# Cached pages laid out by transfers inside SBUF and turned on VectorE, half of a convolution's taps on GpSimd

## What is computed

```python
PAGE_SIZE, KV_LORA, QK_ROPE, N_HEADS, CONV_WIDTH = 128, 256, 32, 16, 31   # 16 pages per sample

def _mla_keys(kv_lat, k_rope, w_uk, g_k_head):
    k_nope = jnp.einsum('btl,lhd->bthd', kv_lat, w_uk)
    k_r = jnp.broadcast_to(k_rope[:, :, None, :], k_nope.shape[:-1] + (QK_ROPE,))
    return _rmsnorm(jnp.concatenate([k_nope, k_r], axis=-1), g_k_head)

# for every page of a sample (kv_blk: 128 tokens x 256, kr_blk: 128 tokens x 32)
k = _mla_keys(kv_blk, kr_blk, w_uk, g_k_head)
sc = jnp.einsum('bshd,bphd->bhsp', qf, k) * scale
# softmax over all pages and the new token, then
acc = jnp.einsum('bhsp,bpl->bhsl', p, kv_blk)

# the convolution of the prompt: 31 taps, each a shifted copy of z times a weight per channel
y = lax.conv_general_dilated(buf, w_dw[:, None, :], ..., feature_group_count=CONV_CH) + b_dw
```

## Time and profile before

| | |
|---|---|
| Median of three runs | 1144.9 us |
| The profiled execution | 1145.37 us |
| Its span on the core | 1143.5 us |
| Busy, share of the span: TensorE, VectorE, ScalarE, GpSimd | 98%, 68%, 51%, 6% |
| Granted TensorE clock, mean | 0.997 |
| Page stage | about 393 to 811 us |

### The profile page before, as it was taken

One profiled execution on the slowest core, in us unless ns is written; L12 is line 12 of the kernel. 1 busy time (PEld: TensorE's weight loads), 2 busy tenths in 40 slices (PEclk: granted clock), 3 DMA queues, 4 the chain that ended last, 5 costly groups with the idle time before them and its releaser, 6 DMA issues.

```text
span 1143.5 us, 25908 instructions
## 1 busy us (share of the span) xinstructions
PE 1122.7 (98%) x9549; PEld 1086.8 (95%) x9549; DVE 778.4 (68%) x1325; ACT 581.7 (51%) x1153; POOL 67.8 (6%) x136
## 2 busy tenths in 40 slices
PE   5999999999999999999999999999999999999998
PEld 3899999999898899999999999999999999999998
DVE  4655553567777688888888888888757666555543
ACT  3444453346576655455545454554566545444432
POOL 2000000010000100101010110101020010000000
PEclk9999999999999999999999999999999999999999
DMA  9987578947344440021211202032257684555552
GB/s 324 314 292 269 183 254 289 348 167 222 99 142 127 133 133 2 20 65 33 52 47 36 62 22 73 13 84 71 57 150 254 227 272 131 183 183 177 177 184 71
DMA packets 165629, 169.84 MB, mean 149 GB/s; under 512 B 25780, under 2 KB 144071, under 8 KB 165525
## 3 DMA queue, kind: packets, MB, share of 16 engines
q1 hardware_dynamic: 163799, 166.83, 45.6%
q10 hardware_dynamic: 1742, 1.88, 0.5%
HBM read 167.13 MB, written 2.49 MB: 148 GB/s over the span
## 4 chain that ended last, share of the span: by engine, by line
PE 92%; DVE 2%; SPq 2%; ACT 1%; DMA 1%; issue 1%; POOL 0%; DVEq 0%; ACTq 0%
PE PS L1894 27%; PE PS L1895 27%; PE PS L1896 27%; PE PS L1971 2%; SPq L451 2%; PE PS L2367 1%; PE PS L2342 1%; PE PS L2343 1%; DMA raw<-in_w_ffn_in 1%; PE PS L2288 1%; PE PS L2099 1%; PE PS L2308 0%; PE PS L2338 0%; DVE wL L1172 0%; PE PS L2287 0%
## 5 line engine op out<-in xcount | busy, mean ns | idle before, releaser
L1172 DVE TENSOR_TENSOR wL<-raw,wH 128x1024 fp32r<-128x1024 f32 (+2 forms) x208 | 246.3, 1191 | 209.8 <-ACT wH L717 208.4
L717 ACT ACTIVATE wH<-raw 128x1024 fp32r<-128x1024 f32 (+2 forms) x208 | 213.2, 1029 | 245.6 <-PE PS L1896 224.7
L1894 PE MATMUL PS<-uH,wH 128*128 128x264 f32 x1024 | 294.2, 287 | 4.5 <-DVE uL L1233 4.0
L1895 PE MATMUL PS<-uL,wH 128*128 128x264 f32 x1024 | 291.8, 285 | 0.0
L1896 PE MATMUL PS<-uH,wL 128*128 128x264 f32 x1024 | 291.4, 285 | 0.0
L1894 PE MATMUL PS<-wqH,kTH 128*128 128x336 f32 (+2 forms) x768 | 255.7, 333 | 0.0
L1896 PE MATMUL PS<-wqH,kTL 128*128 128x336 f32 (+2 forms) x768 | 246.1, 320 | 0.0
L1895 PE MATMUL PS<-wqL,kTH 128*128 128x336 f32 (+2 forms) x768 | 245.9, 320 | 0.0
L1894 PEld LDWEIGHTS PS<-uH,wH 128*128 128x128 f32 x1024 | 193.9, 189 | 7.9 <-issue 6.4
L1895 PEld LDWEIGHTS PS<-uL,wH 128*128 128x128 f32 x1024 | 194.2, 190 | 0.0
L1896 PEld LDWEIGHTS PS<-uH,wL 128*128 128x128 f32 x1024 | 193.6, 189 | 0.0
(11 more groups left out here) (343 smaller groups left out, 1497.8 us busy)
## 6 DMA issues: line engine op xcount, KB each, us to landing
raw<-in_w_ffn_in SPq DMA_DIRECT2D x86, 512.0 KB, 3.5
adaw<-in_w_ada SPq DMA_DIRECT2D x72, 512.0 KB, 6.5
raw<-in_w_ffn_out SPq DMA_DIRECT2D x32, 512.0 KB, 3.5
raw<-in_w_in SPq DMA_DIRECT2D x32, 512.0 KB, 4.5
kv<-in_cache_kv_latent SPq DMA_DIRECT2D x128, 128.0 KB, 2.0
raw<-in_w_ffn_out SPq DMA_DIRECT2D x16, 384.0 KB, 3.0
raw<-in_w_attn_out SPq DMA_DIRECT2D x8, 512.0 KB, 4.1
raw<-in_w_conv_out SPq DMA_DIRECT2D x8, 512.0 KB, 4.7
```

The costliest lines, as they stand in the source:

```text
L717: f(wH[:, k, 0:width], raw[:, k, 0:width], ACT.Copy).then_inc(w_hi, 1)
L1172: v.tensor_tensor(wL[:, k, 0:width], raw[:, k, 0:width], wH[:, k, 0:width].bitcast(F32), ALU.subtract).then_inc(w_lo, 1)
L1894: mm(dst, a[0], b[0], start=start, stop=False)
L1895: mm(dst, a[0], b[1], start=False, stop=False)
```

## The change

- Pages of sequences 1 to 7 are no longer turned by TensorE (`turn` leaves lines 2342 and 2343 out unless `turned`, which holds for sequence 0 only). Instead, for each group of four pages, SP issues four transfers inside SBUF (`blocks`): transfer q takes 32 channels of each half of the four pages, 8 pieces of 32 values (128 bytes) from each of the 128 partitions of `kv2`, and writes them to 32 partitions of a new tile `kx`, 1024 values in each. That is 1024 pieces for a transfer and 4096 for a group. VectorE then turns all blocks of 32 x 32 of `kx` by one instruction on 128 x 1024 into `kT32` (`turn_group`), before `page_lo` of pages 2, 6, 10 and 14, for the group that begins two pages later. `kx` and `kT32` have two slots each and lie where `raw` lies.
- ScalarE (`page_hi`) and VectorE (`page_lo`) read the turned page from `kT32` in SBUF, with an access pattern that puts the tokens in order; the pattern of `kTH` and `kTL` has a step of four values.
- New semaphores: `kx_in` (a group has landed), `kx_ps` (a group is turned), `kr_ps` (rope keys turned and multiplied), which ScalarE, VectorE and GpSimd wait for where they waited for `kT_ps` or `kTH_done`.
- SP's loop over page groups is written out: `sequence_loads(b)` mixes the page loads of the next sequence with the transfers of `blocks`. It starts only after the first gate quad has been split (`w_lo`), and the gate weights of quads 1 to 3 are loaded only after the last `kTL`.
- VectorE does taps 0 to 15 of each tile. GpSimd does taps 16 to 30: a product with the weight (broadcast along the row) and a sum into `yp`, 29 instructions of 128 x 256, in parts of 5, 4, 3 and 3 taps between its other work, and in `conv_sum` one more sum that adds `yp` to the tile.
- `VALUES_PAGE` goes from 10 to 8.

```diff
-VALUES_PAGE = 10
-TAPS = (0, 1, 1, 0, 2, 2, 1, 2, 2, 2, 7, 3, 2, 3, 1, 2)
-TAPS_FIRST = (2, 3, 3, 0, 2, 3, 0, 3, 3, 0, 3, 3, 0, 2, 2, 2)
+VALUES_PAGE = 8
+TAPS = (0, 0, 0, 0, 1, 1, 0, 1, 3, 1, 1, 2, 2, 2, 1, 1)
+TAPS_FIRST = (1, 2, 1, 0, 1, 1, 0, 1, 2, 0, 1, 2, 0, 1, 2, 1)
+DVE_TAPS = sum(TAPS)
+POOL_TAPS = (DVE_TAPS, DVE_TAPS + 5, DVE_TAPS + 9, DVE_TAPS + 12, CW)
...
+        kx = sb("kx", [P, 2, 4 * KL], at=ring)
+        kT32 = sb("kT32", [P, 2, 4 * KL], at=ring + 8192)
+        yp = sb("yp", [P, SEQ], at=gains)
+        ytmp = sb("ytmp", [P, SEQ], at=taps_at)
...
+        def turned_page(n):
+            return kT32[:, n // 4 % 2, :].rearrange("p (k a h t) -> p a h k t", k=4, a=4, h=2)[:, n % 4, :, :, :]
...
+            def pages_next(b, g):
+
+                sp.wait_ge(pg_rel, 4 * b + g + 1)
+                page_group(b, b % 2, g)
+
+            def blocks(b, g):
+
+                grp = 4 * (b - 1) + g
+                sp.wait_ge(kv2_in[4 * (b % 2) + g], 128 * (b // 2) + 128)
+                if grp >= 2:
+                    sp.wait_ge(kx_ps, grp - 1)
+                pages = kv2[:, NPG * (b % 2) + 4 * g:NPG * (b % 2) + 4 * g + 4, :].rearrange(
+                    "p a (h q i) -> p (a h) q i", q=4, i=QUAD)
+                for q in range(4):
+                    sp.dma_start(kx[QUAD * q:QUAD * q + QUAD, grp % 2, :], pages[:, :, q, :]).then_inc(kx_in[grp % 2], 16)
+
+            def sequence_loads(b):
+
+                if b >= 1:
+                    blocks(b, 2)
+                    blocks(b, 3)
+                if 1 <= b < NB - 1:
+                    pages_next(b + 1, 0)
+                if b < NB - 1:
+                    blocks(b + 1, 0)
+                if 1 <= b < NB - 1:
+                    pages_next(b + 1, 1)
+                    pages_next(b + 1, 2)
+                if b < NB - 1:
+                    blocks(b + 1, 1)
+                if 1 <= b < NB - 1:
+                    pages_next(b + 1, 3)
...
-            with sp.Fori(1, 4) as i:
-                sample_pages(i, 0)
-                sample_pages(i, 1)
+            sp.wait_ge(w_lo, 4 * Q_GATE + 4)
+            for b in range(NB):
+                sequence_loads(b)
+            sp.wait_ge(kTL_done, PAGES + 2)
             with sp.Fori(1, 4) as i:
                 gate_quad(i)
...
             def conv_sum(f_):
 
                 pool.wait_ge(tap_done, f_ + 1)
+                own.wait()
+                own.done(g.tensor_tensor(u[:, f_, 0:SEQ], u[:, f_, 0:SEQ], yp[:, :], ALU.add))
+                own.wait()
...
+            def taps(f_, part):
+
+                for t in range(POOL_TAPS[part], POOL_TAPS[part + 1]):
+                    z, w = zbuf[:, f_, t:t + SEQ], wdw[:, f_, t:t + 1].to_broadcast([P, SEQ])
+                    own.wait()
+                    if t == DVE_TAPS:
+                        own.done(g.tensor_tensor(yp[:, :], z, w, ALU.mult))
+                    else:
+                        own.done(g.tensor_tensor(ytmp[:, :], z, w, ALU.mult))
+                        own.wait()
+                        own.done(g.tensor_tensor(yp[:, :], yp[:, :], ytmp[:, :], ALU.add))
...
+            for b in range(NB):
+                taps(b, 0)
+                if b >= 1:
+                    score_max(b - 1)
+                taps(b, 1)
+                if b >= 1:
+                    new_probabilities(b - 1)
+                taps(b, 2)
+                rope_square(b)
+                taps(b, 3)
                 if b < NB - 1:
                     conv_sum(b)
                     sample_rows(b + 1)
+            score_max(NB - 1)
+            new_probabilities(NB - 1)
             conv_sum(NB - 1)
...
-            def page_hi(pg, n):
-                act.wait_ge(kT_ps, pg + 1)
+            def page_hi(b, n, turned=False):
+                pg = NPG * b + n
+                if turned:
+                    act.wait_ge(kT_ps, n + 1)
+                else:
+                    act.wait_ge(kx_ps, 4 * b + n // 4 - 3)
                 act.wait_ge(kn_ps, pg + 1)
...
+                if turned:
+                    f(kTH[:, n % 2, :], PS[:, 0, 0:KL], ACT.Copy).then_inc(kTH_done, 1)
+                else:
+                    f(kTH[:, n % 2, :].rearrange("p (h t k) -> p h k t", h=2, k=4), turned_page(n), ACT.Copy
+                      ).then_inc(kTH_done, 1)
...
+            def turn_group(b, g):
+
+                dve.wait_ge(kx_in[g % 2], 128 * b + 64 * (g // 2) - 64)
+                dve.wait_ge(kTL_done, NPG * b + 4 * g - 2)
+                v.transpose(kT32[:, g % 2, :], kx[:, g % 2, :]).then_inc(kx_ps, 1)
...
+                    v.tensor_tensor(lo_.rearrange("p (h t k) -> p h k t", h=2, k=4), turned_page(n),
+                                    hi_.rearrange("p (h t k) -> p h k t", h=2, k=4), ALU.subtract
+                                    ).then_inc(kTL_done, 1)
...
                 for n in range(NPG):
                     pg = NPG * b + n
+                    if n % 4 == 2:
+                        if n + 2 < NPG:
+                            if not first:
+                                turn_group(b, (n + 2) // 4)
+                        elif not last:
+                            turn_group(b + 1, 0)
                     if not (last and n == NPG - 1):
-                        page_lo(pg + 1, (n + 1) % NPG, b, s, first)
+                        page_lo(pg + 1, (n + 1) % NPG, b, s, first, first and n + 1 < NPG)
...
-                tr(PS[:, 0, 0:128], kv2[:, NPG * s + n, 0:128], ident)
-                tr(PS[:, 0, 128:256], kv2[:, NPG * s + n, 128:256], ident).then_inc(kT_ps, 1)
+                if turned:
+                    tr(PS[:, 0, 0:128], kv2[:, NPG * s + n, 0:128], ident)
+                    tr(PS[:, 0, 128:256], kv2[:, NPG * s + n, 128:256], ident).then_inc(kT_ps, 1)
```

More of the change, by code:

```diff
@@ L169, in decoder_layer @@
         vecT = sb("vecT", [P, V_N])
+        gains = base[0]
         gbc = sb("gbc", [P, B_N])
@@ L356, in decoder_layer @@
         kv2_in = [sem(f"kv2_in{g}") for g in range(8)]
+        kx_ps, kr_ps = sem("kx_ps"), sem("kr_ps")
+        kx_in = [sem(f"kx_in{g}") for g in range(2)]
         qx_done, den_ps, mx_done, gmx_done, sub_done, p_done, lsum_done = map(
@@ L665, in conv_sum, with rope_square @@
                     g.tensor_tensor(ysum[:, :], ysum[:, :], u[:, f_, :], ALU.add).then_inc(ysum_done, 1)
-            pool.wait_ge(st_sb, 4)
-            sample_rows(0)
-            for b in range(NB):
-                pool.wait_ge(kTH_done, NPG * b + 14)
+            def taps(f_, part):
[8 more added lines that the diff above has]
+                        own.done(g.tensor_tensor(yp[:, :], yp[:, :], ytmp[:, :], ALU.add))
+            def rope_square(b):
+                pool.wait_ge(kr_ps, 8 * b + 7)
                 if b >= 1:
@@ L1054, in sequence @@
                     pg = NPG * b + n
-                    if not (last and n == NPG - 1):
-                        page_hi(pg + 1, (n + 1) % NPG)
+                    if n + 1 < NPG:
+                        page_hi(b, n + 1, first)
+                    elif not last:
+                        page_hi(b + 1, 0)
                     if n == 1 and not first:
```

49 lines of the change are left out of this document (27 added, 22 removed).

## The result

| | before | after |
|---|---|---|
| Median | 1144.7 us | 1161.3 us (four runs, 1157.9 to 1164.7) |
| Ratio after to before, 95% interval | | 1.0148 [1.0116, 1.0181] |
| The profiled execution, its span | 1145.37, 1143.5 us | 1164.70, 1162.6 us |
| Granted TensorE clock, mean | 0.997 | 0.990 |

The account below looks back on a forecast made before the run. TensorE, busy 98% of the span, was taken as the bound. Its -24.6 us, plus 5 (lock and heavy pages), 6 (transfers) and 2 (start), gave -11.6: a median of 1133 us, range 1120 to 1155, with 1126 to 1141 at 50%.

Parts of the forecast that it names:

- The 24.6 us from TensorE: Pages 16 to 127: 112 page transpositions of 0.22 us leave TensorE, all on the path; a sequence would last 48.8 us.
- Clean: Rival 1: pieces at 7 to 13 ns, VectorE in time, only 2 us at the start remain: 1122 us; chance 17%.
- kTL at 0.42: VectorE's subtraction in each page, now from SBUF with a stride, left at 0.42 us, bounds 0.35 and 0.6.
- The lock: GpSimd and VectorE block each other at shared SBUF ports: 36 exposed operations, 4.5 us more VectorE per sequence.
- the heavy pages: VectorE at pages 2, 6, 10, 14, with the lock: 0.7 us per sequence reaches TensorE, 5 us, bounds 0 and 25.
- The transposition: VectorE's new 128x1024 instruction, four a sequence: 1.14 us each, bounds 0.6 and 2.4, 4.6 us a sequence.
- Its maximum: GpSimd's maximum over partitions: reached 14 us into the sequence, VectorE asks at 17, so covered by 3 us.
- The transfers, "which I think decide": SP's 128-byte-piece transfers at 15 ns a piece arrive 1.0 us late in sequences 2 to 7: 6 us, bounds 0 and 36.
- B + L: Issue time plus landing time of a sequence's second transfer group: 8.4 us taken, may be 7.4 without making VectorE late.
- Once at the start: First transfers wait for the gate weights' low half and land late for VectorE: 1 to 3 us, 2 taken.
- Slower by the transfers: Rival 2: at 27 ns a piece, six sequences each wait 6 us at page 2: 1163 us; chance 17%.
- slower by the lock: Rival 3: every exposed VectorE operation waits out half a GpSimd operation, VectorE needs 54 us a sequence: 1160 us; chance 7%.

Follow-up runs that it names:

- e9b: Kernel after without GpSimd's taps and the stride, gate pages earlier, and without transfers inside SBUF but the first two groups of sequence 1: 1129.3 us.
- e4: Kernel after without GpSimd's 15 taps, with contiguous rows (token order not restored) and gate pages at 3, 5, 7, 9 of sequence 0: 1147.0 us.
- e3: Kernel after with the first gate weights split at pages 3, 5, 7, 9 of sequence 0, not 3, 6, 9, 12; computes everything: 1154.3 us.
- e10b: Kernel after with gate pages earlier and without transfers inside SBUF but the first two groups; GpSimd's taps and the stride stay: 1149.7 us.
- e13: Half of the change: pages 8 to 15 by transfers and two token-ordering transpositions, values at page 10, 9 taps on GpSimd: 1143.2 us.

## Why the prediction was wrong

1. **The 24.6 us from TensorE.** The instructions went as said. Without transfers, stride and lock 16.2 come through (e9b), 8.4 less. "Clean" (1122) was out of reach even there. The two sequences with a turn are together 4.5 us longer than the others, where before it was 0.7, and each undisturbed sequence is 0.9 us longer than the forecast 48.8, 0.3 of it a visible stop for kTL. The prediction had no term for the turns.
2. **kTL at 0.42: the step that failed.** "The subtraction kTL reads SBUF and not PSUM, with a stride; I leave it at 0.42, bounds 0.35 and 0.6" was a choice without a row for a stride. It measured 0.61 with the stride alone, just over the upper bound, and 0.72 with the lock. ScalarE's copy kTH was not priced at all; it went from 0.41 to 0.68. That ScalarE's copy from SBUF could be it stood only in the last sentence. The prediction had the right frame for it: 1.2 us of cover from the earlier trace rows, 1.0 without the transpositions. With 0.27 and 0.19 more for kTH and kTL, that is 0.5, before any lock, and behind the transpositions at pages 2, 6 and 14 it isn't enough. The stride alone costs 10.3 us where 0 was forecast.
3. **The lock.** In VectorE's time the forecast held: 36 operations, 4.5 us in a sequence. Measured are 16 x 0.11 for kTL (0.61 to 0.72) and 16 x 0.17 for the taps (0.48 to 0.65 over all of them), 4.5 us. The mistake was what it costs TensorE: 5 us for it and the heavy pages together; 6.0 alone and 10.1 beside the stride (20.4 less 10.3). Stride and lock together, 20.4, still lie inside the bounds of 0 and 25 that the term had; 5 was the wrong choice between them. And the 0.72 us tap of the earlier trace rows ended 0.28 after GpSimd's product, sooner than the 0.48 of a tap that waits out all of it: it showed that a tap is held up, not for how long. VectorE's work of 48.6 is the forecast 45.6 plus the stride's 16 x 0.19 = 3.0.
4. **The transposition** was taken at 1.14 and took 1.23, 1.16 from start to start: right. GpSimd's total was forecast at 30 us and was 28.2. Its maximum was late once, by 0.6 us, so on time as said, but with less to spare than 3 us: the 6 us that it takes ahead of its record were in no row that I had read. The 7 behind it were, in the earlier trace rows, as the 7.4 idle before L665, and I passed over them.
5. **The transfers, "which I think decide".** They don't, in the kernel after: 4.5 us, near the 6 of the sum by luck, as they hide behind a late VectorE. Alone they cost 17.7. From the window at 443 to 449, 106 GB/s in pieces of 128 bytes are 1.21 ns a piece, 19.3 ns per piece and engine; 15 was taken. With 19.3, B + L is 2.4 + 402 x 0.0193 = 10.2 us, 2.8 over the budget of 7.4, 17 us for six sequences: with the right pace the prediction's own formula lands at what e4 less e9b measured. That is partly luck: the six waits in e4 were 1.9 us on average and not 2.8, and part of the cost came by a lower clock (0.990 in e4, 0.995 in e9b), which the formula doesn't have. The Trainium skill ("DMA: Bandwidth & Descriptors", section "Why small descriptors are slow (HBM only)") says that transfers from SBUF to SBUF don't suffer the penalty of small descriptors; its example is a remote transfer with 128-byte packets. This trace doesn't agree for transfers inside one core's SBUF: 106 GB/s in pieces of 128 bytes, beside the 300 GB/s of the earlier trace rows in pieces of 512.
6. **Once at the start.** 2 us were forecast and 7.1 measured (after less e3). The group landed 7.3 us after the gate's last low half, where 4 to 6 was taken. TensorE's stop was 4.0, and 3 more went to the half clock behind it. The prediction had no term for the clock anywhere; in the profiled execution it comes to some 8 us.
7. **The sum again**, by the runs: -24.6 + 8.4 (not reached in e9b) + 20.4 (stride and lock) + 4.5 (transfers on top) + 7.1 (start) = +15.8, against +16.6 measured. That it closes proves nothing: e9b, e10b, e3 and the kernel after are a chain in which each term is the difference of two neighbours, and the 0.8 is what the kernel before differs by between chips. In another order the shares would be others, as costs here don't add.
8. **The rivals.** "Slower by the transfers" (1163) and "slower by the lock" (1160) both named nearly the time, by luck. The first took 27 ns a piece; the pace was 19.3, just under its own threshold of 20, and the cause was another. The second had the right place and asked for 0.31 us per exposed operation; the lock gave 0.13 (4.5 over 36), and the stride, which no rival had, the rest.

## What to carry to other kernels

When work moves from a bounding engine to a chain of others, write down that chain for one unit of work (here kTH, kTL, TensorE's start) and price every operation in it anew with its new operands and access patterns; a busy share says nothing of it. Where a price has no row, take the bound that hurts: two strides of 0.2 to 0.3 us in a chain with 1.0 us of cover cost 10 us by themselves, and left the transfers only 4.5 to add. Moving only so much that the old cover stands (half the pages, five taps, GpSimd's work where VectorE reads PSUM) kept 7 us of 12, where the whole change lost 17.

## What the hardware showed that I had not expected

- Writing 128x256 with a step of four values, and reading in pieces of 32: ScalarE 0.68 us, 0.43 on contiguous SBUF rows; VectorE, with one input in the stepped order too, 0.61 against 0.41. The transposition of 128x1024 went from 1.23 to 2.01 when it wrote with such a step.
- TensorE's granted clock was 0.50 for 6 us after its stop of 4.0 us (443 to 449, after) and 0.52 for 3 us after a stop of 2.0 (549 to 552, e9b), though TensorE was working again. After the stop of 1.6 us at the other turn in e9b it stayed at 1.00 (648 to 655). The stop of 4.0 us thus cost 7 (7.1 by the kernel after less e3).
- GpSimd's maximum over partitions, 0.39 us by its record, keeps the engine for some 13 us when other work stands on both sides of it (5.8 and 6.8 us of "issue" in e13).
- The turn of the loop leaves VectorE 1.5 to 3.3 us without an instruction (1.5 and 1.7 before, 2.8 and 3.3 in e9b). It cost little before, where TensorE had work ahead, and cost e9b about 4 us.
- Costs of engines that feed one chain don't add: stride and lock 10.3 and 6.0 alone, 20.4 together; transfers 17.7 alone, 4.5 behind the two.
